# Compression of a paged cache: the loop over batch rows unrolled and staggered by component, both chunk halves summed in one PSUM bank, and small vectors of the front loaded as rows

## The chip, the cores and the metric

The kernel runs on one NeuronCore of one Trainium2 chip. The metric is the device time of one launch in microseconds (us), the median of several runs; lower is better.

## What is computed

One decoder layer for a prompt of 1024 tokens and for 8 samples of one token, each with 4096 cached tokens in pages. Two of its parts matter here. The **front** makes modulation vectors from the conditioning (`silu(c) @ w_ada + b_ada`), normalizes the tokens, modulates them and multiplies them by the input projection; a short convolution over three tokens follows on a part of its columns. The **compression** turns each 32 cached raw key or value rows (stride 16) into one row by a small MLP:

```python
chunks = kv_raw.reshape(B, n_chunk, 16, 2, N_KV_HEADS, 64)
w1 = cmp_w1.reshape(2, CMP_CHUNKS, 16, 64, 128)          # CMP_CHUNKS = 2 halves
proj = einsum('bnsckd,crsdh->bnrckh', chunks, w1)
hid = proj[:, :n, 0] + proj[:, 1:n + 1, 1]                # half 0 of a chunk + half 1 of the next
bias = einsum('cld,cldh->ch', cmp_pos, cmp_w1) + cmp_b1
hid = gelu(hid + bias)
comp = einsum('bnckh,chd->bnckd', hid, cmp_w2) + cmp_b2   # keys are rotated afterwards
```

It runs for 8 samples (256 chunks each) and for the prompt (64 chunks). There are four components for each: key or value, times two heads. Attention, a mixture of experts and the final norm follow and aren't touched.

## The kernel before

The kernel is a row of stages with a barrier between them: `fro` (the front), `cmp` (compression), `att`, `smp`, the merge and routing, `moe`, `fin`. Each engine has its own program; they meet at semaphores. fp32 numbers are split into a high part (`h`, type fp32r) and a remainder (`l`), and each product is three fp32r matmuls.

**Front (`stage_front`).** SP loads four 2 MB pieces of `w_ada` (three buffers), then pieces of `w_in`. POOL loads the nine token tiles (512 KB each) into four buffers; between tiles 2 and 3 it issues five loads of small vectors (`biasT`, `gT`, `wconv`) as columns, elements of 4 bytes. PE makes `condition(n)` (16 fp32 matmul instructions), then transposes two token tiles, four times; the last, 8-row tile comes at the end. ACT and DVE then split the first 8 blocks of weights, and ACT makes the modulated high part `xh` with scale and bias in one pass while DVE makes the modulated fp32 value and the remainder `xl`. 12 convolution groups and 27 groups of `z` (three blocks of columns, nine token tiles) follow. The results of `z` go out through two buffers, so group m waits for the store of group m-2 (L609). The last rows for the convolution state leave from POOL as six transfers of 4-byte elements (L300, L302).

**Compression (`stage_compress`).** For sample i, POOL gathers two halves of 128 chunks, 2 MB each, into `x0`, `x1`. ACT and DVE copy them into `xs` by component (`shuffle`); PE transposes 4 blocks at a time into one of four banks (16 such groups for a sample, L901); ACT copies each to `xh` (L768), DVE writes the remainder `xl` (L838) and thereby frees the bank. `product` is 48 fp32r matmuls of 256 columns (L911) for a component; the two chunk halves go to two parts of a bank, and DVE adds them with a shift of one column (L846, L848), then ACT makes the gelu (L786). `second` is the fp32 product with `w2`: for keys two matmuls, the second with rotated columns (L881, L882), for values one for each half (L887). `keys` and the rows at L855 finish the output. The order within a sample is written out:

```python
return (turn[0:8] + nxt[0:1] + turn[8:12] + [("product", 0)] + turn[12:14] + [("product", 1)]
        + turn[14:16] + nxt[1:2] + [("product", 2), ("product", 3)])
```

Sample 0 is unrolled, 1 to 7 are in a hardware loop (the last one partly outside, on ACT and DVE), and the prompt is a ninth pass with 64 columns. Before all this SP loads the page table in eight pieces and the positions as columns (4-byte elements), then tables and weights, the first-layer weight `w1` (2 MB) last, and right behind it a 4 MB copy in HBM (`o_win_s`). PE makes the position bias with 32 fp32 matmuls of one column (L869).

## Time and profile before

| what | value |
|---|---|
| median of 3 runs | 2507.45 us (2501.72 to 2516.19) |
| the profiled execution | 2502.97 us |
| its span, first to last instruction | 2501.2 us |
| mean granted TensorE clock | 0.876 |
| front | 0 to 349 us |
| compression, set-up until its first product | 352 to 418 us |
| compression, 8 samples | 418 to 725 us |
| compression, prompt | 725 to 773 us |

The profiled execution is one run; what is worked out from its rows is measured against its own time. Busy time of PE is modelled (matmuls are pipelined), so the distance between the starts of two matmuls is the better measure of their cost. PEclk is the share of full clock that was granted: 1.00 is 2.4 GHz, 0.50 is 1.2 GHz.

### The profile page before, as it was taken

To read this page: it belongs to the slowest core of one execution; us is meant where nothing else is said; L and a number is where in the kernel's file an instruction comes from. 1 tells how busy PE (TensorE), PEld (TensorE's weight loads), DVE (VectorE), ACT (ScalarE), POOL (GpSimd) and SP (SyncE) were. 2 spreads that over 40 slices of the span, in tenths; PEclk is the share of its full clock that TensorE was granted. 3 is DMA by queue.
4 is the path that set the end of the run, shared out by engine and by line. 5 is a ranking of instruction groups with operands and counts; after the bars stand their busy time and mean duration, and the time that the engine had idled before them with its cause. 6 is when DMAs were issued, how large, how long until landed. Compare 5 with 4: busy or idle time off the path is not lost. (4 is left out here: it accounts for less than half of the span.)

```text
span 2501.2 us, 29798 instructions
## 1 busy us (share of the span) xinstructions
...
## 2 busy tenths in 40 slices
...
GB/s 271 95 70 16 84 111 202 117 128 113 58 5 87 228 23 17 5 5 17 129 164 225 33 299 89 77 48 320 425 426 415 415 416 411 415 335 275 194 52 287
DMA packets 168247, 444.13 MB, mean 178 GB/s; under 512 B 49157, under 2 KB 96227, under 8 KB 136397
## 3 DMA queue, kind: packets, MB, share of 16 engines
...
q14 instruction: 34, 0.28, 0.0%
...
## 5 line engine op out<-in xcount | busy, mean ns | idle before, releaser
L2626 DVE TENSOR_TENSOR moe_lo<-wts_raw,moe_hi 128x2048 fp32r<-128x2048 f32 x216 | 484.4, 2287 | 59.8 <-ACT moe_hi L2541 59.7
L2541 ACT ACTIVATE moe_hi<-wts_raw 128x2048 fp32r<-128x2048 f32 x216 | 401.3, 1915 | 25.2 <-PE moe_U L2423 25.2
L911 PE MATMUL cmp_hp<-cmp_xh,cmp_wh 128*128 128x256 f32 (+1 forms) x576 | 177.0, 307 | 16.5 <-DVE cmp_xl L838 16.5
L911 PE MATMUL cmp_hp<-cmp_xh,cmp_wl 128*128 128x256 f32 (+1 forms) x576 | 174.0, 302 | 0.0
L911 PE MATMUL cmp_hp<-cmp_xl,cmp_wh 128*128 128x256 f32 (+1 forms) x576 | 173.9, 302 | 0.0
L2409 PE MATMUL moe_G<-moe_hi,moe_xh 128*128 128x512 f32 x288 | 117.6, 408 | 44.0 <-DVE moe_lo L2626 36.3
L2449 PE MATMUL moe_Y<-moe_hi,moe_hh 128*128 128x512 f32 x288 | 118.6, 412 | 29.4 <-DVE moe_hl L2642 24.9
L911 PEld LDWEIGHTS cmp_hp<-cmp_xh,cmp_wh 128*128 128x128 f32 x576 | 122.9, 213 | 21.8 <-issue 19.2
L1309 ACT ACTIVATE att_prow<-att_S,att_low 128x640 f32<-128x640 f32 (+15 forms) x192 | 107.7, 563 | 46.5 <-DVE att_low L1367 43.8
L1299 ACT ACTIVATE att_ph<-att_pT 128x512 fp32r<-128x512 f32 (+5 forms) x148 | 88.3, 597 | 87.1 <-PE att_pT L1207 86.8
L911 PEld LDWEIGHTS cmp_hp<-cmp_xh,cmp_wl 128*128 128x128 f32 x576 | 123.1, 214 | 0.0
L911 PEld LDWEIGHTS cmp_hp<-cmp_xl,cmp_wh 128*128 128x128 f32 x576 | 123.1, 214 | 0.0
L1352 DVE TENSOR_TENSOR att_pl<-att_pT,att_ph 128x512 fp32r<-128x512 f32 (+5 forms) x148 | 101.5, 689 | 35.7 <-ACT att_ph L1299 33.6
L2450 PE MATMUL moe_Y<-moe_hi,moe_hl 128*128 128x512 f32 x288 | 116.9, 406 | 0.0
L2451 PE MATMUL moe_Y<-moe_lo,moe_hh 128*128 128x512 f32 x288 | 116.5, 405 | 0.0
L2410 PE MATMUL moe_G<-moe_hi,moe_xl 128*128 128x512 f32 x288 | 116.2, 404 | 0.0
L2411 PE MATMUL moe_G<-moe_lo,moe_xh 128*128 128x512 f32 x288 | 116.1, 403 | 0.0
L786 ACT ACTIVATE cmp_hid<-cmp_raw,cmp_bias 128x255 f32<-128x255 f32 (+1 forms) x36 | 17.7, 491 | 231.5 <-DVE cmp_raw L848 231.5
L2421 PE MATMUL moe_U<-moe_hi,moe_xh 128*128 128x512 f32 x288 | 115.0, 399 | 0.0
L2423 PE MATMUL moe_U<-moe_lo,moe_xh 128*128 128x512 f32 x288 | 112.4, 390 | 0.0
L2422 PE MATMUL moe_U<-moe_hi,moe_xl 128*128 128x512 f32 x288 | 112.3, 390 | 0.0
L1367 DVE TENSOR_REDUCE att_low<-att_S 128x1 f32<-128x640 f32 (+14 forms) x184 | 98.3, 547 | 20.9 <-PE att_S L1240 19.3
...
## 6 DMA issues: line engine op xcount, KB each, us to landing
...
```

What stands on the lines that cost most here:

```text
L911: last = pe.matmul(hp[k % 2][:, r, 0:cols], lhs[:, w, :], rhs[:, k, t, 0:cols], start=(t == 0 and m == 0), stop=(t == 7 and m == 2))
L2409: pe.matmul(G[:, :], xh[k][:, c, :], wh, start=(c == 0), stop=False)
L2410: pe.matmul(G[:, :], xl[k][:, c, :], wh, start=False, stop=False)
L2411: last = pe.matmul(G[:, :], xh[k][:, c, :], wl, start=False, stop=(c == KT - 1))
L2421: pe.matmul(U[:, :], xh[k][:, c, :], wh, start=(c == 0), stop=False)
L2422: pe.matmul(U[:, :], xl[k][:, c, :], wh, start=False, stop=False)
L2423: last = pe.matmul(U[:, :], xh[k][:, c, :], wl, start=False, stop=(c == KT - 1))
L2449: pe.matmul(Y[part][:, :], hh[:, c, :], wh, start=(c == 0), stop=False)
L2450: pe.matmul(Y[part][:, :], hl[:, c, :], wh, start=False, stop=False)
L2451: last = pe.matmul(Y[part][:, :], hh[:, c, :], wl, start=False, stop=(c == KD - 1))
L2541: act.activation(hi[p][half][:, :], raw[p][half][:, :], ACT.Copy).then_inc(hi_ready[p], 1)
L2626: dve.tensor_tensor(lo[p][half][:, :], raw[p][half][:, :], hi[p][half][:, :], ALU.subtract).then_inc(lo_ready[p], 1)
```

## The change

In the front, the small vectors and the convolution's weights arrive as 36 rows and are transposed by PE (`cols`, `colT`); they and `state_conv` are issued behind the first `w_ada` piece, and token tiles 2 and 3 wait for that piece. Token tiles are transposed 2, 3, 3 and 1 at a time. The modulation is made by DVE alone (`modulate`), ACT then only copies the high part. The ends of the convolution are gathered in `endT`, transposed by PE after the first group of `z`, copied by ACT and stored by SP as rows.

In the compression, 32 steps u = 4i + c (sample, component) are unrolled. In step u PE does `product(u)`, then `turn(u + 2)` and `second(u - 1)`; the copies for u + 4 follow. `xh` and `xl` hold three components. Both chunk halves accumulate in one bank, the second reading its columns one element later (`t * TS + r`). The positions are two extra columns of steps 0 and 2, the prompt's 64 chunks are extra columns of the last four steps (320 in all). Keys take one matmul of 128 output rows. The page indices are spread by a small matmul; `w1` comes as two halves in the gather buffer of sample 1 and is loaded early; the copy `o_win_s` is issued after sample 0.

The diff, cut:

```diff
-        biasT = s.sb("biasT", [P, 2 * KT])
-        gT = s.sb("gT", [P, KT])
+        NCOL = 3 * KT + 3 * CJ
+        cols = s.sb("cols", [NCOL, P])
+        colT = s.sb("colT", [P, NCOL])
+        biasT, gT = colT[:, 0:2 * KT], colT[:, 2 * KT:3 * KT]
+        wconv = colT[:, 3 * KT:NCOL].rearrange("p (r j) -> p r j", r=3)
         modT = s.sb("modT", [P, 2 * KT, 9])
...
-            for n in range(NRAW):
+            load_raw(0)
+            sp.dma_start(cols[0:2 * KT, :], a["b_ada"][0, 0:2 * D].rearrange("(k p) -> k p", p=P)).then_inc(st_in, 16)
+            sp.dma_start(cols[2 * KT:3 * KT, :], a["ln1_g"][0].rearrange("(k p) -> k p", p=P)).then_inc(st_in, 16)
+            sp.dma_start(cols[3 * KT:NCOL, :], a["w_conv"][0].rearrange("r (j p) -> (r j) p", p=P)).then_inc(st_in, 16)
+            sp.dma_start(st[:, :], a["state_conv"][0].rearrange("b r n -> (b r) n")).then_inc(st_in, 16)
+            for n in range(1, NRAW):
                 load_raw(n)
-            sp.dma_start(st[:, :], a["state_conv"][0].rearrange("b r n -> (b r) n")).then_inc(st_in, 16)
             for n in range(NRAW, ADA1 + NRAW):
...
+            sp.wait_ge(tails_kept, 1)
+            sp.dma_start(a["o_conv_p"][0, 0], ends[0:2, :]).then_inc(row_out, 16)
+            sp.dma_start(a["o_conv_s"][0, :, 1, :], ends[2:2 + NB, :]).then_inc(row_out, 16)
...
+                if t == 2:
+                    pool.wait_ge(w_in[0], 16)
                 if t >= 4:
                     pool.wait_ge(turned, t - 3)
                 src = a["x_prompt"][0, t * P:(t + 1) * P, :] if t < NT else a["x_sample"][:, 0, :]
                 pool.dma_start(x[t % 4][0:n, :], src).then_inc(x_in[t % 4], 16)
-                if t == 2:
-                    with nc.allow_non_contiguous_dma(reason="columns of small vectors"):
-                        pool.dma_start(biasT[:, :], a["b_ada"][0, 0:2 * D].rearrange("(k p) -> p k", p=P)).then_inc(const_in, 16)
-                        pool.dma_start(gT[:, :], a["ln1_g"][0].rearrange("(k p) -> p k", p=P)).then_inc(const_in, 16)
-                        for r in range(3):
-                            pool.dma_start(wconv[:, r, :], a["w_conv"][0, r].rearrange("(j p) -> p j", p=P)).then_inc(const_in, 16)
...
-            pool.wait_ge(tails, CJ)
-            with nc.allow_non_contiguous_dma(reason="rows of conv state"):
-                for r in range(2):
-                    pool.dma_start(a["o_conv_p"][0, 0, r].rearrange("(j p) -> p j", p=P), tail[:, :, r]).then_inc(end_out, 16)
-                for j in range(CJ):
-                    pool.dma_start(a["o_conv_s"][0, :, 1, j * P:(j + 1) * P].rearrange("b p -> p b"), vsT[:, j, :]
-                                   ).then_inc(end_out, 16)
-            pool.wait_ge(end_out, 16 * (2 + CJ))
...
+        turns = [(0, 1), (2, 3, 4), (5, 6, 7), (8,)]
...
-            act.wait_ge(kept_v, TT)
-            act.wait_ge(mod_ready, 2)
+            for k in range(KT):
+                act.wait_ge(h_ready, k + 1)
+                act.activation(xh[:, k, 0:T], raw[:, k, 0:T], ACT.Copy).then_inc(h_high, 1)
+            act.wait_ge(h_ready, KT + 1)
             act.activation(xh[:, :, T:W], raw[:, :, T:W], ACT.Copy).then_inc(h_high, 1)
-            for k in range(KT):
-                act.activation(xh[:, k, 0:T], raw[:, k, 0:T], ACT.Identity, bias=modT[:, k, NB:9],
...
-                turn(2 * n)
-                turn(2 * n + 1)
+                for t in turns[n]:
+                    turn(t)
...
+            def modulate(k):
+                dve.tensor_scalar(raw[:, k, 0:T], raw[:, k, 0:T], modT[:, KT + k, NB:9], modT[:, k, NB:9],
+                                  ALU.mult, ALU.add).then_inc(h_ready, 1)
+                dve.wait_ge(h_ready, k + 1)
+
+            modulate(0)
+            for k in range(KT):
+                if k + 1 < KT:
+                    modulate(k + 1)
+                else:
+                    step(dve.tensor_tensor(raw[:, :, T:W], raw[:, :, T:W], modT[:, KT:, 0:NB], ALU.mult))
+                    dve.tensor_tensor(raw[:, :, T:W], raw[:, :, T:W], modT[:, 0:KT, 0:NB], ALU.add).then_inc(h_ready, 1)
+                    dve.wait_ge(h_ready, KT + 1)
+                dve.wait_ge(h_high, k + 1)
+                dve.tensor_tensor(xl[:, k, 0:T], raw[:, k, 0:T], xh[:, k, 0:T], ALU.subtract).then_inc(h_split, 1)
...
+    def cols(u):
+
+        if u in (0, 2):
+            return NCH + 2
+        return NCH if u < NU - 4 else TS
+
...
+    order = [("shuffle", 0), ("shuffle", 1), ("turn", 0), ("turn", 1), ("shuffle", 2), ("shuffle", 3)]
+    for u in range(NU):
+        order.append(("product", u))
+        if u + 2 < NU:
+            order.append(("turn", u + 2))
+        if u + 4 < NU:
+            order.append(("shuffle", u + 4))
...
+        x = [[s.sb(f"x{i}{h}", [P, 16 * 4 * HD]) for h in range(2)] for i in range(2)]
+        xs = [[s.sb(f"xs{i}{h}", [P, 16, HD]) for h in range(2)] for i in range(2)]
+        xp = s.sb("xp", [PCH, 4, 16, HD])
+        xh = s.sb("xh", [P, 3, 8 * TS + 2], F32R)
+        xl = s.sb("xl", [P, 3, 8 * TS + 2], F32R)
...
-            return (turn[0:8] + nxt[0:1] + turn[8:12] + [("product", 0)] + turn[12:14] + [("product", 1)]
-                    + turn[14:16] + nxt[1:2] + [("product", 2), ("product", 3)])
...
+            sp.dma_start(pages[:, :], a["page_table"]).then_inc(page_in, 16)
+            sp.dma_start(ident[:, :], a["c_ident"]).then_inc(page_in, 16)
+            sp.dma_start(spread[:, :, :], a["c_pages"]).then_inc(page_in, 16)
+            sp.dma_start(c8[:, :], a["c_mod8"]).then_inc(page_in, 16)
+            sp.dma_start(pos[:, :], a["cmp_pos"][0].rearrange("c (t l) d -> (c t) (l d)", l=2)).then_inc(page_in, 16)
+            for k in range(2):
+                sp.dma_start(w1[:, 16 * k:16 * k + 16, :],
+                             a["cmp_w1"][0, k].rearrange("(t l) d h -> (l d) t h", l=2)).then_inc(w_in[k], 16)
...
+            prompt = a["o_cmp_p"][0, 0].rearrange("(n s) k g d -> n (k g) s d", s=16)
+            for c in range(4):
+                sp.dma_start(xp[:, c, :, :], prompt[:, c, :, :]).then_inc(prompt_in, 16)
+            for b in range(NB):
+                if b == 1:
+                    sp.dma_start(a["o_win_s"][0, :, 0:511].rearrange("b (x y) c g d -> b x (y c g d)", y=7),
+                                 a["cache_win_kv"][0, :, 1:512].rearrange("b (x y) c g d -> b x (y c g d)", y=7)
+                                 ).then_inc(win_out, 16)
...
+                    if i == 1 and h == 0:
+                        pool.wait_ge(w_split, 2)
+                    if i >= 2:
+                        pool.wait_ge((shuffled_a, shuffled_v)[h], 4 * (i - 2) + 4)
+                    pool.indirect_dma_start(x[i % 2][h][:, :], None, chunks,
+                                            bass.IndirectOffsetOnAxis(ap=idx[:, h, i:i + 1], axis=0)).then_inc(x_in[i % 2][h], 16)
...
+            def second(u):
+                i, c = u // 4, u % 4
+                n = max(NCH, cols(u)) if i else NCH
+                pe.wait_ge(hid_ready, u + 1)
+                if c < 2:
+                    pe.wait_ge(k_done, 2 * i + c)
+                    pe.matmul(kp[:, 0:n], w2k[:, :], hid[:, u % 2, 0:n], start=True, stop=True).then_inc(k_psum, 1)
...
+            def product(u):
+                c = u % 4
+                n = cols(u)
+                pe.wait_ge(free, turned_to(u))
+                if u >= 2:
+                    pe.wait_ge(hid_ready, u - 1)
+                if u == 0:
+                    pe.wait_ge(pos_ready, 1)
+                if u in (0, 2):
+                    pe.wait_ge(w_split, u // 2 + 1)
+                for r in range(2):
+                    for t in range(8):
+                        w = 16 * (c // 2) + 8 * r + t
+                        at = slice(t * TS + r, t * TS + r + n)
+                        for m, (lhs, rhs) in enumerate(((wh, xh), (wl, xh), (wh, xl))):
+                            last = pe.matmul(hp[u % 2][:, 0:n], lhs[:, w, :], rhs[:, u % 3, at],
+                                             start=(r == 0 and t == 0 and m == 0), stop=(r == 1 and t == 7 and m == 2))
+                last.then_inc(product_done, 1)
...
+            for what, n in order:
+                if what == "turn":
+                    turn(n)
+                    if n == 2:
+                        pe.wait_ge(const_in, 16 * NCONST)
+                        pe.wait_ge(w2_ready, 1)
+                    elif n > 2:
+                        second(n - 3)
+                elif what == "product":
+                    product(n)
+                    if n + 2 >= NU:
+                        second(n - 1)
...
+            def keep(v):
+                for m, (v_, h, t0) in enumerate(turns):
+                    if v_ != v:
+                        continue
+                    act.wait_ge(turned, m + 1)
+                    if v >= 3:
+                        act.wait_ge(product_done, v - 2)
+                    n = parts(v)[h]
+                    copy(xv[:, v % 3, t0:t0 + 4, h * P:h * P + n], bank[m % 4][:, :, 0:n]).then_inc(high, 1)
...
+            def gelu(u):
+                i, c = u // 4, u % 4
+                n = cols(u) if i else NCH
+                act.wait_ge(product_done, u + 1)
+                if u in (0, 2):
+                    act.wait_ge(bias_ready, u // 2 + 1)
+                if u >= 2:
+                    j, d = (u - 2) // 4, (u - 2) % 4
+                    act.wait_ge((k_psum, v_psum)[d // 2], 2 * j + d % 2 + 1)
+                act.activation(hid[:, u % 2, 0:n], hp[u % 2][:, 0:n], ACT.Gelu_apprx_tanh, bias=bias[:, c // 2:c // 2 + 1]
+                               ).then_inc(hid_ready, 1)
...
-                        dve.tensor_copy(raw[k % 2][:, 0:n], hp[k % 2][:, 0, 0:n]).then_inc(added, 1)
-                        dve.wait_ge(added, 4 * i + k + 1)
-                        dve.tensor_tensor(raw[k % 2][:, 0:n], raw[k % 2][:, 0:n], hp[k % 2][:, 1, 1:n + 1],
-                                          ALU.add).then_inc(raw_ready, 1)
```

**DVE in the compression.** Before, from the transposed groups before the first product to the one before the third (`cmp_xl` is the remainder, `cmp_raw` the sum of the halves):

```order
L838 TENSOR_TENSOR cmp_xl<-cmp_bank,cmp_xh 128x4x128 x8
L706 COPY cmp_xs<-cmp_x 128x1024 x2
L838 TENSOR_TENSOR cmp_xl<-cmp_bank,cmp_xh 128x4x128 x4
L846 COPY cmp_raw<-cmp_hp 128x255
L848 TENSOR_TENSOR cmp_raw<-cmp_raw,cmp_hp 128x255
L838 TENSOR_TENSOR cmp_xl<-cmp_bank,cmp_xh 128x4x128 x2
L846 COPY cmp_raw<-cmp_hp 128x255
L848 TENSOR_TENSOR cmp_raw<-cmp_raw,cmp_hp 128x255
L838 TENSOR_TENSOR cmp_xl<-cmp_bank,cmp_xh 128x4x128 x2
L706 COPY cmp_xs<-cmp_x 128x1024 x2
```

Now, two steps behind one another (`cmp_t`, `cmp_ck` finish keys, `cmp_cv` values, `cmp_xs` is the copy by component):

```order
L924 SCALAR_TENSOR_TENSOR cmp_t<-cmp_kp,cmp_b,cmp_rope 64x256
L926 SCALAR_TENSOR_TENSOR cmp_t<-cmp_kp,cmp_b,cmp_rope 64x256
L928 TENSOR_TENSOR cmp_ck<-cmp_t 64x256
L917 TENSOR_TENSOR cmp_xl<-cmp_bank,cmp_xh 128x4x128 x4
L737 COPY cmp_xs<-cmp_x 128x1024
L924 SCALAR_TENSOR_TENSOR cmp_t<-cmp_kp,cmp_b,cmp_rope 64x256
L926 SCALAR_TENSOR_TENSOR cmp_t<-cmp_kp,cmp_b,cmp_rope 64x256
L928 TENSOR_TENSOR cmp_ck<-cmp_t 64x256
L917 TENSOR_TENSOR cmp_xl<-cmp_bank,cmp_xh 128x4x128 x4
```

The twelve remainders ahead of a product are gone from there; each step has four remainders and one copy for later steps, and the two adding instructions on `cmp_raw` no longer exist.

**SP at the head of the compression.** Before:

```order
L714 DMA cmp_pt<-in_page_table 16x16x1 x8
L715 DMA cmp_pos<-in_cmp_pos 128x32x1
L716 DMA cmp_b<-in_cmp_b 128x2x1
L718 DMA cmp_b<-in_cmp_b 64x1
L719 DMA cmp_b<-in_cmp_b 32x1
L720 DMA cmp_b<-in_cmp_b 32x1
L721 DMA cmp_ident<-in_c_ident 128x128
L722 DMA cmp_rope<-in_c_ropec 64x510
L723 DMA cmp_b2v<-in_cmp_b 128x64
L724 DMA cmp_w<-in_cmp_w 128x2x64
L725 DMA cmp_w<-in_cmp_w 128x32x128
L727 DMA o_win_s<-in_cache_win_kv 8x8x16352
```

Now, behind the page table, the identity, the spreading table and `c8`:

```order
L745 DMA cmp_pos<-in_cmp_pos 32x128
L747 DMA cmp_x<-in_cmp_w 128x16x128 x2
L750 DMA cmp_b<-in_cmp_b 128x2x1
L752 DMA cmp_b<-in_cmp_b 64x1
L753 DMA cmp_b<-in_cmp_b 32x1
L754 DMA cmp_b<-in_cmp_b 32x1
L755 DMA cmp_rope<-in_c_ropec 128x320
L756 DMA cmp_b2v<-in_cmp_b 128x64
L757 DMA cmp_w<-in_cmp_w 128x2x64
L758 DMA cmp_w2k<-in_cmp_w 128x32
L759 DMA cmp_w2k<-in_cmp_w 128x32
L762 DMA cmp_xp<-o_cmp_p 64x16x64 x4
```

`w1` (`in_cmp_w` 128x16x128, twice) moved ahead of the small tables, the column loads of pages and positions are gone, four loads of the prompt's rows are new, and the copy `o_win_s` is no longer here.

**PE at the end of the front's first part** (`fro_wraw` x8 is `condition`, `fro_xbuf` a token tile, `fro_mrow` the modulation). Before:

```order
L406 MATMUL fro_tp<-fro_ident,fro_xbuf 128x128 x16
L413 MATMUL fro_ps<-fro_ident,fro_mrow 128x9 x4
L396 MATMUL fro_ps<-fro_wraw,fro_cT 9x512 x8
L406 MATMUL fro_tp<-fro_ident,fro_xbuf 128x128 x16
L413 MATMUL fro_ps<-fro_ident,fro_mrow 128x9 x8
L406 MATMUL fro_tp<-fro_ident,fro_xbuf 128x8 x8
L439 MATMUL fro_ps<-fro_xh,fro_wh 128x344
```

Now:

```order
L398 MATMUL fro_ps<-fro_wraw,fro_cT 9x512 x8
L408 MATMUL fro_tp<-fro_ident,fro_xbuf 128x128 x24
L415 MATMUL fro_ps<-fro_ident,fro_mrow 128x9 x4
L398 MATMUL fro_ps<-fro_wraw,fro_cT 9x512 x8
L408 MATMUL fro_tp<-fro_ident,fro_xbuf 128x8 x8
L415 MATMUL fro_ps<-fro_ident,fro_mrow 128x9 x8
L441 MATMUL fro_ps<-fro_xh,fro_wh 128x344
```

Two more token tiles stand ahead of the last `condition`, and the small one now stands ahead of the last turns of the modulation, whose end the first product waits for.

## Rows read from the trace of the kernel before

**Rows 1.** The page of the kernel before, its first line.

```profile
span 2501.2 us, 29798 instructions
```

**Rows 2.** Compression by stage: window, length, busy time (instructions) of PE to POOL, PEclk, DMA, GB/s.

```profile
504.50:527.00 22.50, 21.42 (x170) 19.93 (x167) 9.70 (x22) 5.94 (x10) 0.94 (x1) 1.00 0.27 100
527.00:538.50 11.50, 9.21 (x64) 7.36 (x65) 8.92 (x16) 8.34 (x15) 0.94 (x1) 0.97 0.17 40
725.00:773.00 48.00, 47.03 (x238) 46.05 (x237) 7.21 (x26) 4.45 (x12) 0.00 (x0) 0.51 0.02 4
```

**Rows 3.** DVE in order of time, compression: start, us, line, names, x, [idle before].

```profile
425.74 0.42 DVE L846 COPY cmp_raw<-cmp_hp 128x255 f32<-128x255 f32 x1 [6.42 <-PE cmp_hp L911]
...
432.36 0.42 DVE L846 COPY cmp_raw<-cmp_hp 128x255 f32<-128x255 f32 x1 [3.39 <-PE cmp_hp L911]
...
701.67 0.42 DVE L846 COPY cmp_raw<-cmp_hp 128x255 f32<-128x255 f32 x1 [6.47 <-PE cmp_hp L911]
...
723.08 0.42 DVE L846 COPY cmp_raw<-cmp_hp 128x255 f32<-128x255 f32 x1 [4.69 <-PE cmp_hp L911]
```

**Rows 4.** PE in order of time, compression, four places.

```profile
418.18 0.43 PE L911 MATMUL cmp_hp<-cmp_xh,cmp_wh 128*128 128x256 f32 x1 [2.00 <-DVE cmp_xl L838]
418.41 0.42 PE L911 MATMUL cmp_hp<-cmp_xh,cmp_wl 128*128 128x256 f32 x1
...
428.20 0.28 PE L911 MATMUL cmp_hp<-cmp_xh,cmp_wh 128*128 128x256 f32 x1
428.32 0.28 PE L911 MATMUL cmp_hp<-cmp_xh,cmp_wl 128*128 128x256 f32 x1
...
510.72 0.64 PE L881 MATMUL cmp_kp<-cmp_hid,cmp_w 128*64 128x255 f32 x2
511.20 0.59 PE L882 MATMUL cmp_kp<-cmp_hid,cmp_w2r 128*64 128x255 f32 x2
...
728.91 0.40 PE L911 MATMUL cmp_hp<-cmp_xl,cmp_wh 128*128 128x64 f32 x1
729.12 0.40 PE L911 MATMUL cmp_hp<-cmp_xh,cmp_wh 128*128 128x64 f32 x1
```

**Rows 5.** Groups by line and shape, compression, ACT and DVE: xcount, busy us, mean ns.

```profile
L768 ACT ACTIVATE cmp_xh<-cmp_bank 128x512 fp32r<-128x512 f32 x128 | 69.2, 597 | 23.6 <-PE cmp_bank L901 23.6
L768 ACT ACTIVATE cmp_xs<-cmp_x 128x1024 f32<-128x1024 f32 x32 | 32.0, 1054 | 25.4 <-DMA cmp_x<-in_cache_cmp_kv,cmp_idx 25.4
L786 ACT ACTIVATE cmp_hid<-cmp_raw,cmp_bias 128x255 f32<-128x255 f32 x32 | 16.3, 509 | 189.7 <-DVE cmp_raw L848 189.7
...
L838 DVE TENSOR_TENSOR cmp_xl<-cmp_bank,cmp_xh 128x512 fp32r<-128x512 f32 x128 | 79.8, 684 | 28.7 <-ACT cmp_xh L768 28.6
L706 DVE COPY cmp_xs<-cmp_x 128x1024 f32<-128x1024 f32 x32 | 20.6, 686 | 14.2 <-DMA cmp_x<-in_cache_cmp_kv,cmp_idx 14.2
```

**Rows 6.** The same stage view over 50 us of the front, 344 columns a matmul.

```profile
100.00:150.00 50.00, 50.00 (x320) 50.00 (x319) 22.10 (x49) 10.01 (x20) 0.00 (x0) 1.00 0.22 75
```

**Rows 7.** ACT in order of time at the head of the compression.

```profile
370.08 2.00 ACT L768 ACTIVATE cmp_xs<-cmp_x 128x1024 f32<-128x1024 f32 x2 [21.65 <-DMA cmp_x<-in_cache_cmp_kv,cmp_idx]
375.82 2.00 ACT L768 ACTIVATE cmp_xs<-cmp_x 128x1024 f32<-128x1024 f32 x2 [3.73 <-DMA cmp_x<-in_cache_cmp_kv,cmp_idx]
393.90 3.62 ACT L773 ACTIVATE cmp_wh<-cmp_w 128x4096 fp32r<-128x4096 f32 x1 [16.08 <-DMA cmp_w<-in_cmp_w]
```

**Rows 8.** PE in order of time at the beginning of the front.

```profile
17.90 9.26 PE L396 MATMUL fro_ps<-fro_wraw,fro_cT 128*9 128x512 f32 x16 [12.88 <-DMA fro_wraw<-in_w_ada]
...
71.47 0.62 PE L439 MATMUL fro_ps<-fro_xh,fro_wh 128*128 128x344 f32 x1 [9.25 <-DVE fro_xl L551]
```

**Rows 9.** PE in order of time between two groups of z.

```profile
268.68 0.76 PE L439 MATMUL fro_ps<-fro_wh,fro_xh 128*128 128x512 f32 x1 [6.26 <-DVE fro_wl L509]
```

**Rows 10.** Waits of DVE between 220 and 300 us: total, times, longest.

```profile
DVE fro_arena L609 <- DMA s_z<-fro_arena: 26.0, 2, 20.4
```

**Rows 11.** The stage view over four us after the stop of group 9.

```profile
268.00:272.00 4.00, 3.32 (x9) 2.69 (x10) 4.00 (x7) 0.00 (x0) 0.00 (x0) 0.55 0.18 70
```

475 lines of the change are left out of this document (218 added, 257 removed).

## The prediction

> **What bounds the kernel now.** I read the page first, then the stage view, to see where TensorE (PE) is full and where it waits. The span is 2501.2 us [rows 1]; the profiled execution took 2502.97 us, 4.5 us below the median of 2507.45 us. The stages are separated by barriers, so time taken out of the front or the compression goes out of the total one for one, and the stages behind stay as they are.
>
> The compression has three faults of its own. (1) Its nine passes are not full. The reader should take the start of the first adding copy of sample 0, 425.74, and of sample 7, 701.67: seven samples in 275.93 us, 39.4 us each [rows 3]. Inside a sample PE is full from 504.5 to 527, at full clock, while from 527 to 538.5 it is busy 9.2 of 11.5 us with transposes that wait for ACT and DVE [rows 2]. (2) The prompt's pass takes 48 us, with PE busy 47 of them at a granted clock of 0.51 [rows 2]: its matmuls start 0.21 us apart though they have only 64 columns, no faster than 256 columns at the low clock, 0.23 us [rows 4]. (3) The head: the gathered halves are there at 370.08 and 375.82, but the weight lands at 393.90 [rows 7], and the first product starts at 418.18 [rows 4].
>
> In the front, PE has nothing to multiply until the first piece of `w_ada` lands at 17.90, and the first projection matmul is at 71.47 [rows 8]. Later DVE waits 26.0 us in two waits for stores of `z` [rows 10], is late with a weight split, and PE stands 6.26 us [rows 9], after which the mean clock over four us is 0.55 [rows 11].
>
> **The steps of the compression.** A matmul of 256 columns costs 0.12 us [rows 4], so one product is 48 x 0.12 = 5.76 us. Between the adding copies of components 0 and 1 lie 6.62 us [rows 3], that is one product and 8 transposes, so 8 transposes cost 0.86 us and the 16 of a component 1.72 us. A key's second matmul costs 0.48 us (510.72 to 511.20 [rows 4]); one of two goes. For a value's four narrow matmuls I take the same 0.5. A component then needs 5.76 + 1.72 + 0.5 = 7.98 us of PE. Before, four components needed about 4 x 7.98 + 2 x 0.48 = 32.9 us of the 39.4.
>
> PE reaches these 7.98 us only if nothing in a step is late. ACT does four copies, one shuffle and one gelu: 4 x 0.60 + 1.05 + 0.51 = 3.9 us. DVE does four remainders and one shuffle, 4 x 0.68 + 0.69 = 3.4 us, and an output of up to three instructions of a size with the copy of rows 3, 0.42 us, 4.7 in all [rows 5]. Both are well inside 7.98, and the order gives them a whole product of lead: turns run two components ahead, their bank is freed during the product, the gelu that `second` needs is a product old, and the two adding instructions on DVE have gone. The adding itself I count as no gain: its 0.84 us a component are DVE's, beside a product of 5.76; only if DVE became the bound would its going be worth that much. The gathers (4 MB for 32 us) are doubled, so each has a sample's time; two 2 MB halves came 5.74 us apart [rows 7]. The 4 MB copy blocks SP's queue behind sample 0's stores; SP's next duty is the store of sample 1's keys, some 30 us later.
>
> Sum from the first product: 32 x 5.76 = 184.3; turns 30 x 1.72 = 51.6 (two are ahead of the first product); second 32 x 0.5 = 16. The prompt's 64 extra columns: 344 columns cost 50 / 320 = 0.156 us [rows 6], so 64 more columns cost 0.026 us, times 192 = 5.0; its transposes 1.7 (between 0 and 3.4, the price of full ones). The start at the low clock: 418.18 to 425.74 is 7.56 instead of 5.76, so 1.8. The last output 1.9, as from 723.08 to 725 now [rows 2, 3]. Together **262.3 us** against 773 - 418.2 = 354.8 now: **-92.5**.
>
> The head: `w1` is issued some ten us earlier on SP, ahead of the small tables, and without the 4 MB copy; 2 MB cost about 5.7 us. The indices take one more hop (two transposes and a matmul on PE), against eight column loads less. So the last wait becomes the second gathered half. It can come at 372 (less traffic) or at 382 (the prompt's rows, 1 MB in small pieces, beside it); I keep the 375.8 of now plus 1. Behind it are two DVE copies, four remainders and the turns between: 2 x 0.69 + 4 x 0.68 and a us for PE, 5 us. The position bias on PE, the long split and 48 transposes are no longer between. First product at 382 instead of 418.2: **-36** (-31 to -41).
>
> **The steps of the front.** The first `w_ada` piece shares the DMA engines with two token tiles instead of four and with none of the element loads: 3 MB at 5.7 us for 2 MB is 8.6 us, from about 3.5, so it lands at 12 instead of 17.9. I take -5.5 (0 if the elements cost nothing, at most -9). PE's work after it is the same but for one small transpose; the last tile moves ahead of the final modulation turn, and DVE's `modulate(0)` replaces a wait for ACT: -0.5. The products that follow are PE's own pace. In `z` the element stores are gone, DVE is no longer late: -6.3, and -1.8 of clock (4 us at 0.55 [rows 11]); four transposes more, +0.4. The ends of the convolution wait for one group of `z` on ACT, which has nothing else there, and SP's first store of `z` waits about as long for its own group. Front: **-13.7** (-5 to -18).
>
> Total -92.5 - 36 - 13.7 = -142. 2503 - 142 = 2361; the median lies 4.5 higher, so **2365 us**.
>
> **The rivals.**
> - *A step has a hidden wait.* A handshake each step (PE's first bank, the gelu's wait for the matmul two steps back, a wait on DVE's chain) of 1 us costs 32 us: 2397. For it: PE lost about 2 us in 527 to 538.5 to this very chain [rows 2]; against it: the lead of one product.
> - *The clock falls in the turns.* Rows 2 show 1.00 over 22.5 us with 16 transposes between products, and 0.97 where 48 transposes stood with gaps, so I don't expect it. If each turn let it fall, a step would lose the 1.8 us of a cold start [rows 3, 4]: 32 x 1.8 = 58, so 2423. The Trainium skill ("TensorE: Matmul & The Clock Gate", Part 4: PE-mode transpose) says that transposes don't count as work for the clock; by that rule the time would be this one, and the trace speaks against it in short turns.
> - *The shifted half is read at half rate.* The second half's columns start one element on, which no matmul here does now. If it costs double: 24 x 32 x 0.12 = 92, so 2457.
> - *It falls into the slow gear: slower than before.* The 64-column matmuls show such a gear: 0.21 us for 64 columns at the low clock [rows 2, 4], four times the price of a column. At full clock 256 columns would cost 0.21 x 4 / 2 = 0.42, 0.30 more, times 768 = 230 us: 2595. It decides from 142 / 768 = 0.185 us more a matmul. Nothing in the trace hints at it but the gear itself; 256 columns and more aren't in it.
> - *The head and front move little.* Loads land no earlier than now because the rate and not the order bounds them: `w_ada` at 17.9 and the second half at 387. 5.5 + 11 less, so 2382.
>
> **How the numbers follow.** Forecast 0.76, hidden wait 0.08, clock 0.06, half rate 0.03, slow gear 0.03, early loads 0.04. The range 2342 to 2400: down by 5 of the head, 4 of the front, 2 of the turns and 12 for steps closer than my distances (0.4 us each, as a value's second product can be half); up to the hidden wait and the late loads. The clock, half rate and gear stay outside, 0.12, and some 0.08 of the forecast's tails. About 0.5% (12.5 us) is what a measurement can tell from no change. Faster by more: all but the gear, 0.97. The gear near its point of decision gives 0.01 for the same, the rest 0.02 slower.
>
> **What would show it.** Right: the first product of the compression about 36 us earlier after the front's end, adding copies gone, `product` every 8.0 us, PEclk 1.00 throughout, the last four products 7.0 us each, PE's wait in `z` gone, compression 292 us from 352 (421 now). Wrong: a step well over 8.2 us (see which wait), matmuls of the shifted half further apart than 0.12, a clock under 1.00 in the turns, the first product waiting for `w1` or for the prompt's rows, or ACT waiting long for a gather.

## The result and the profile after

The changed kernel takes 2383.64 us (median of 4 runs, 2378.95 to 2386.85), the kernel before beside it on the same chip 2511.0 us (4 runs, 2501.72 to 2516.19). The ratio is 0.949 with a 95% interval of 0.946 to 0.952. The forecast was 2365 us with a range of 2342 to 2400; it holds, 18.6 us above the point. The profiled execution took 2384.1 us, where the sum had said 2361.

The page of the kernel after, its first line; it answers to [rows 1]:

```profile
span 2382.3 us, 28748 instructions
```

The stage view of the kernel after: the end of the head, the start of the products, and the steps up to the prompt's (window, length, busy time and instructions of PE, PEld, DVE, ACT, POOL, then PEclk, DMA share, GB/s). It answers to [rows 2]:

```profile
366.00:371.70 5.70, 5.02 (x24) 5.02 (x25) 5.18 (x8) 2.84 (x5) 0.00 (x0) 0.50 1.16 327
371.70:380.00 8.30, 8.30 (x68) 8.30 (x67) 2.86 (x7) 4.15 (x6) 1.87 (x2) 0.94 1.09 359
...
420.00:604.00 184.00, 183.35 (x1537) 181.94 (x1536) 89.40 (x176) 78.28 (x138) 9.03 (x8) 1.00 0.32 121
```

PE is full from the first product on. In the 184 us from 420 on it stands 0.65 us, at a granted clock of 1.00, though 16 transposes lie between any two products. The stretch of 48 us at 0.51 is gone: the prompt's 64 columns ride in the bank of the last sample. The rival of the clock falling in the turns is answered in this view alone.

The gelus of the kernel after in order of time (start us, length, engine, line, shapes, count, idle before). One stands behind each product, so their distance is a step:

```profile
441.44 0.47 ACT L892 ACTIVATE cmp_hid<-cmp_hp,cmp_bias 128x256 f32<-128x256 f32 x1 [4.49 <-PE cmp_hp L841]
...
584.20 0.47 ACT L892 ACTIVATE cmp_hid<-cmp_hp,cmp_bias 128x256 f32<-128x256 f32 x1 [4.48 <-PE cmp_hp L841]
...
593.58 0.47 ACT L892 ACTIVATE cmp_hid<-cmp_hp,cmp_bias 128x256 f32<-128x256 f32 x1 [5.07 <-PE cmp_hp L841]
...
604.21 0.53 ACT L892 ACTIVATE cmp_hid<-cmp_hp,cmp_bias 128x320 f32<-128x320 f32 x1 [6.33 <-PE cmp_hp L841]
...
614.87 0.53 ACT L892 ACTIVATE cmp_hid<-cmp_hp,cmp_bias 128x320 f32<-128x320 f32 x1 [7.37 <-PE cmp_hp L841]
...
625.66 0.53 ACT L892 ACTIVATE cmp_hid<-cmp_hp,cmp_bias 128x320 f32<-128x320 f32 x1 [7.49 <-PE cmp_hp L841]
633.22 0.53 ACT L892 ACTIVATE cmp_hid<-cmp_hp,cmp_bias 128x320 f32<-128x320 f32 x1 [7.04 <-PE cmp_hp L841]
```

From 441.44 to 584.20 lie 18 steps: 7.93 us each, forecast 7.98. In these steps, of samples 2 to 6, nothing else sets the pace; `[4.48 <-PE cmp_hp L841]` is ACT waiting for PE. With the prompt's columns a step takes 10.6 to 10.8 us, and the last, which has no turns beside it, 7.56.

The head, in order of time over all engines; it answers to [rows 4, 7]:

```profile
340.04 0.28 DVE L624 TENSOR_TENSOR fro_arena<-fro_arena 8x128 f32<-8x128 f32 x1
...
352.34 1.91 ACT L871 ACTIVATE cmp_wh<-cmp_x 128x2048 fp32r<-128x2048 f32 x1 [12.98 <-DMA cmp_x<-in_cmp_w]
...
358.34 1.91 ACT L871 ACTIVATE cmp_wh<-cmp_x 128x2048 fp32r<-128x2048 f32 x1 [4.09 <-DMA cmp_x<-in_cmp_w]
...
360.83 2.00 ACT L871 ACTIVATE cmp_xs<-cmp_x 128x1024 f32<-128x1024 f32 x2 [0.58 <-DMA cmp_x<-in_cache_cmp_kv,cmp_idx]
...
365.93 1.30 DVE L737 COPY cmp_xs<-cmp_x 128x1024 f32<-128x1024 f32 x2 [3.35 <-DMA cmp_x<-in_cache_cmp_kv,cmp_idx]
...
371.72 0.56 PE L841 MATMUL cmp_hp<-cmp_xh,cmp_wh 128*128 128x258 f32 x1
```

The gathered halves land at 360.83 and 365.93 and the first product starts at 371.72 (418.18 before, [rows 4]). The weight's halves land at 352.34 and 358.34 and are split before the second gathered half is there, so the weight is off the path.

The front: PE in order of time; it answers to [rows 8]:

```profile
12.46 9.64 PE L398 MATMUL fro_ps<-fro_wraw,fro_cT 128*9 128x512 f32 x16 [7.54 <-DMA fro_wraw<-in_w_ada]
...
34.37 1.06 PE L408 MATMUL fro_tp<-fro_ident,fro_xbuf 128*128 128x128 f32 x8 [0.83 <-DVE fro_arena L507]
37.20 1.06 PE L408 MATMUL fro_tp<-fro_ident,fro_xbuf 128*128 128x128 f32 x8 [1.77 <-ACT fro_arena L323]
...
51.58 8.73 PE L398 MATMUL fro_ps<-fro_wraw,fro_cT 128*9 128x512 f32 x16
```

`w_ada` lands at 12.46 instead of 17.90. But the third transposes of a group wait 1.77 us (and 1.75 once more, in the next group), and the last modulation product takes 8.73 us where it took 7.04, as this line of the kernel before shows:

```profile
50.81 7.04 PE L396 MATMUL fro_ps<-fro_wraw,fro_cT 128*9 128x512 f32 x16
```

The first projection matmul starts at 69.45, only 2.0 us earlier than in [rows 8].

Between the compression's last output and the next stage, all engines in order of time:

```profile
635.51 0.48 DVE L936 TENSOR_TENSOR cmp_cv<-cmp_vp,cmp_b2v 128x64 f32<-128x64 f32 x3 [1.07 <-PE cmp_vp L823]
636.01 0.65 SPq L772 DMA_DIRECT2D s_cv<-cmp_cv  x2
636.71 0.96 SPq L773 DMA_DIRECT2D s_ck<-cmp_ck  x1
637.71 0.51 SPq L774 DMA_DIRECT2D s_cv<-cmp_cv  x1
...
642.56 0.06 DVE L1463 MEMSET att_ckt<- 128x2 f32 x1 [6.58 <-PEq L84]
```

DVE waits 6.58 us for the next stage. In the kernel before, at the same place:

```profile
775.45 0.06 DVE L1402 MEMSET att_ckt<- 128x2 f32 x1 [2.57 <-PEq L84]
```

The last stores stand behind the last output, and the stage ends when they have landed. There are four now (64.0, 63.5, 31.5 and 31.5 KB); before there was one of 31.5 KB.

Stage by stage, against the profiled execution of the kernel before (PE's last matmul of the front, DVE's last output of the compression, PE's first and last turning matmul of the attention, PE's first projection matmul of the merge, DVE's last output; each read from the tile's own view):

| stage | before | after | difference |
|---|---|---|---|
| front, to PE's last matmul | 347.8 | 338.7 | -9.1 |
| compression, to its last output | 424.9 | 297.1 | -127.8 |
| to the attention's first matmul | 9.6 | 13.5 | +3.9 |
| attention of the prompt | 388.6 | 395.4 | +6.8 |
| attention of the samples | 298.3 | 303.9 | +5.6 |
| merge, experts, final | 1027.5 | 1028.8 | +1.3 |

The two parts that the change touches most gave 136.9 us, and 17.6 of them are gone behind them, 12.4 in two stages whose instructions are the same. Where those went is what most of the experiments are about.

### The profile page after: what moved, and what is told of

Its sections match the earlier page's. It is cut to its first block and busy times, and to the rows that moved or that the text cites. A ratio compares the mean times of both kernels' runs of the same rounds, so it can differ in the third digit from the quotient of the medians.

```text
span 2382.3 us, 28748 instructions
## 1 busy us (share of the span) xinstructions
PE 1986.7 (83%) x10585; PEld 1579.7 (66%) x10585; DVE 1341.0 (56%) x2058; ACT 1052.4 (44%) x1605; POOL 110.6 (5%) x107
## 5 line engine op out<-in xcount | busy, mean ns | idle before, releaser
L917 DVE TENSOR_TENSOR cmp_xl<-cmp_bank,cmp_xh 128x512 fp32r<-128x512 f32 (+1 forms) x136 | 82.6, 668 | 121.1 <-ACT cmp_xh L871 121.0
L841 PE MATMUL cmp_hp<-cmp_xh,cmp_wh 128*128 128x256 f32 (+2 forms) x512 | 150.5, 294 | 0.0
L841 PE MATMUL cmp_hp<-cmp_xh,cmp_wl 128*128 128x256 f32 (+2 forms) x512 | 147.0, 287 | 0.0
L841 PE MATMUL cmp_hp<-cmp_xl,cmp_wh 128*128 128x256 f32 (+2 forms) x512 | 146.9, 287 | 0.0
L1428 DVE TENSOR_REDUCE att_low<-att_S 128x1 f32<-128x640 f32 (+14 forms) x184 | 98.7, 548 | 21.7 <-PE att_S L1301 18.9
L441 PE MATMUL fro_ps<-fro_xh,fro_wh 128*128 128x344 f32 x288 | 93.6, 325 | 9.9 <-DVE fro_xl L565 8.0
L1268 PE MATMUL att_pT<-att_ident,att_prow 128*128 128x128 f32 (+7 forms) x592 | 98.5, 292 | 3.8 <-DVE att_pl L1413 2.5
L841 PEld LDWEIGHTS cmp_hp<-cmp_xh,cmp_wh 128*128 128x128 f32 x512 | 97.7, 191 | 0.5
```

The lines of the kernel that those rows point to most:

```text
L841: last = pe.matmul(hp[u % 2][:, 0:n], lhs[:, w, :], rhs[:, u % 3, at], start=(r == 0 and t == 0 and m == 0), stop=(r == 1 and t == 7 and m ...
```

## The experiments

Twelve further runs were made in three groups, each group on one chip with the kernel before beside it, which took 2520.2, 2518.1 and 2515.6 us; times are best read as ratios.

### The two parts alone

The compression as changed with the front as it was: function `stage_front` of the kernel before in the changed kernel.

> The compression as changed, the front as it was. By the two traces the compression's last output came 136.9 us earlier and the front's end 9.1 us earlier, so the compression itself gained 127.8 us; some 4 us of it went back at the stage's end, where the last stores are now waited for. Theory A: the 14 us that the attention and sample stages took longer in the changed kernel's profile are their own (the granted clock there varies from one execution to the next), so the gain against the kernel before is 124 us give or take 6, and the stages of this run show another pattern of clock than either. Theory B: the loss comes with the compression's new end (what it leaves in the queues, or the clock it leaves behind): the gain is 110 us and the same stages show the same dips of the clock as in the changed kernel. Theory C: it comes with the front; then 124 us here with the clock of the kernel before in those stages.

The ratio was 0.950 (0.948 to 0.952), 2395.6 us against 2520.2: -124.6. That is the number of theories A and C, and B's 110 is outside the interval (121 to 132 us). C wanted the clock of the kernel before in the later stages, but the attention took 400.2 us in this trace and 388.6 in that one, so A is left. The reverse, `stage_front` of the changed kernel in the kernel before:

> The front as changed, the compression as it was. Theory A: 9 us less than the kernel before (between 6 and 12, since the front ended 9.1 us earlier and nothing behind it is bound to it). Theory B: the two parts lean on each other (the loads of the compression follow the front's last stores), so the two single gains don't add up to the gain of the whole, 127 us. If the later stages' clock is a matter of where in time they begin, this run, 9 us ahead of the kernel before, may show dips that neither other run has.

The ratio was 0.993 (0.991 to 0.995), 2504.6 us: -15.6, more than the 9 us expected, with an interval that reaches from 12.9 to 21.7 us (0.9949 and 0.9914 times 2520.2). In its trace the front ended at 341.1, 6.7 us earlier than in the kernel before, so the rest lies behind the front; what made it is not shown, the later stages' own scatter (below) is large enough. The sum of both, 140 us, stands against a gain of the whole of 127 us in the first comparison and 136 in the repeat below; with intervals of 4 to 9 us to either side of each number this shows no loss from putting the two together.

### The pace of the steps

Does the lead of one product fill PE, or would one bank and fewer adding copies have done it?

```
-    order = [("shuffle", 0), ("shuffle", 1), ("turn", 0), ("turn", 1), ("shuffle", 2), ("shuffle", 3)]
+    order = [("shuffle", 0), ("shuffle", 1)]
     for u in range(NU):
+        order.append(("turn", u))
+        if u + 2 < NU:
+            order.append(("shuffle", u + 2))
         order.append(("product", u))
-        if u + 2 < NU:
-            order.append(("turn", u + 2))
-        if u + 4 < NU:
-            order.append(("shuffle", u + 4))
```

> The changed kernel with the order turn, shuffle, product: the turns of a component stand right ahead of its own product, with no component between. Theory A (the pipelining is what fills PE): in the changed kernel the last remainder of a component ends 3.8 us after its first transpose, and the product could start 2.0 us after it, so PE would stand about 1.8 us in each of 31 steps: 56 us, 2440 us in place of 2384 (2425 to 2460, the upper end if the standing lets the clock fall, 1.8 us more in some steps); the head is some 3 us shorter, as only one component is turned ahead. Theory B (the gain comes from fewer adding copies and one bank, the lead does nothing): under 10 us more.

It took 2431.0 us, a ratio of 0.966 (0.962 to 0.970), 48.7 us more than the changed kernel on that chip, where 56 were expected; 2431 lies in the stated 2425 to 2460. The waits of PE in its compression, from 378 to 695 us (engine, line, what it waited for: us in total, times, longest):

```profile
PE cmp_hp L840 <- DVE cmp_xl L916: 47.1, 31, 4.5
```

31 waits of 1.5 us in the mean, 47.1 in all, for the last remainder: theory A. A step took 9.68 us (19 steps between the gelus at 410.58 and 594.52) instead of 7.93, 1.75 more, where 1.8 had been expected. To its last output the compression took 358.5 us instead of 297.1, so the order is worth 61.4 us of the stage by the traces; the whole shows 48.7 because the two later stages were short in this run (691.0 us together, 699.7 in the changed kernel's repeat). Whether the waits cost clock as well:

```profile
380.00:420.00 40.00, 32.46 (x248) 31.41 (x249) 15.34 (x29) 12.74 (x23) 2.19 (x2) 0.91 0.30 111
420.00:600.00 180.00, 151.21 (x1241) 145.96 (x1241) 73.81 (x143) 65.37 (x114) 10.94 (x10) 1.00 0.38 147
600.00:640.00 40.00, 33.93 (x269) 32.85 (x268) 15.20 (x31) 13.76 (x24) 0.00 (x0) 0.96 0.03 7
640.00:696.00 56.00, 50.12 (x349) 46.69 (x348) 18.56 (x43) 15.12 (x31) 0.00 (x0) 0.97 0.03 8
```

Over 180 us they did not, at 1.00 with PE busy in 151.2 of 180 us; at both ends the clock stood at 0.91, 0.96 and 0.97, where the changed kernel has 1.00.

The other half of the question, the adding copies put back between product and gelu:

```
-                act.wait_ge(product_done, u + 1)
+                act.wait_ge(raw_ready, u + 1)
...
+                    dve.wait_ge(product_done, n + 1)
...
+                    step(dve.tensor_copy(raw[:, n % 2, 0:m], hp[n % 2][:, 0:m]))
+                    dve.tensor_tensor(raw[:, n % 2, 0:m], raw[:, n % 2, 0:m], hp[n % 2][:, 0:m], ALU.max).then_inc(raw_ready, 1)
```

> The changed kernel with two DVE instructions between each product and its gelu put back, a copy out of the bank and a maximum with the bank (which leaves the values as they are), as the kernel before had a copy and an addition there. Theory A (the adding copies were never the cost, the lead hides them): 32 x 0.84 = 27 us more of DVE beside PE, and the time the same within 0.3%. Theory B (their going is part of the gain): up to 27 us more, 2411. If the turns' copies on ACT, which stand behind the gelu, get late, PE shows waits at the transposes of some 0.8 us in each component; that is theory B's sign.

The ratio was 0.949 (0.943 to 0.955), the median 2388.7 us, and the interval is too wide for 0.3%. The trace says more than the time. Its groups by line and shape, from 378 to 635 us (counts, busy us, mean ns, idle before), and PE's waits there:

```profile
L987 DVE COPY cmp_raw<-cmp_hp 128x256 f32<-128x256 f32 x28 | 11.9, 424 | 54.3 <-PE cmp_hp L843 54.3
L988 DVE TENSOR_TENSOR cmp_raw<-cmp_raw,cmp_hp 128x256 f32<-128x256 f32 x28 | 11.8, 421 | 1.0
```

```profile
PE cmp_bank L812 <- DVE cmp_xl L919: 4.5, 4, 1.2
```

DVE does 26.7 us more (with 3.0 us for the three of 320 columns), and PE waits 4.5 us in four waits, all for a free bank at the turns with the prompt's rows, which are six groups on four banks. From the first product to the last it took 267.5 us against 261.2: the two instructions cost 6.3 us of 27. Nearly all of it is in the steps with the prompt's rows: the 18 steps from the gelu at 441.94 to that at 584.75 take 7.93 us each, as without them. Theory A holds for the steps without the prompt, B for the four steps where a turn waits for DVE.

The odd first column:

```
-                        at = slice(t * TS + r, t * TS + r + n)
+                        at = slice(t * TS, t * TS + n)
```

> The changed kernel with the second half of each product read from the same first column as the first half, not one on; so the position of a token half within a chunk is wrong in the compressed keys and values, everything else is computed as before. Theory A (an odd first column costs nothing): the matmuls of 256 columns start 0.118 us apart as now, a component 7.86 us, the same time within 0.3%. Theory B (it costs something that the even spacing hides, such as a first access of two): 768 matmuls by 5 ns or more, at least 4 us less.

The ratio was 0.944 (0.939 to 0.949), too wide again, but the products span 260.8 us in its trace and 261.2 in the changed kernel's: 0.5 ns a matmul. The shifted half costs nothing.

### The front

The same tiles, turned in pairs:

```
-        turns = [(0, 1), (2, 3, 4), (5, 6, 7), (8,)]
+        turns = [(0, 1), (2, 3), (4, 5), (6, 7, 8)]
```

> The changed kernel with the token tiles turned in pairs, as before, and the last group of three with the short tile at its end. Theory A: the groups of three are what ate the front's gain. ACT squares and scales a tile between two copies, so the third turn of a group waited 1.77 and 1.75 us; with pairs each group waits 0.83, which gives back 2.7 us, and the modulation product before the last turns goes from 8.73 to 7.04 us as its clock is whole again: some 4 us less than the changed kernel, the front's first weight split at 57 us instead of 61. Theory B: the token tiles come late because they wait for the first piece of the modulation weight, and the turns would wait in pairs as well: no change, within 1 us. Theory C: the short tile's turn at the end costs what the pairs give.

2376.7 us, a ratio of 0.942 (0.941 to 0.944). The kernel was not run beside the changed one, so its front is read from its trace, PE in order of time:

```profile
34.61 1.06 PE L408 MATMUL fro_tp<-fro_ident,fro_xbuf 128*128 128x128 f32 x8 [0.83 <-DVE fro_arena L507]
...
46.17 7.04 PE L398 MATMUL fro_ps<-fro_wraw,fro_cT 128*9 128x512 f32 x16
...
55.06 1.07 PE L408 MATMUL fro_tp<-fro_ident,fro_xbuf 128*128 128x128 f32 x8 [0.83 <-DVE fro_arena L507]
56.96 0.63 PE L408 MATMUL fro_tp<-fro_ident,fro_xbuf 8*128 8x8 f32 x8 [0.83 <-DVE fro_arena L507]
```

No wait over 0.83 us, 7.04 us for the last modulation product, and the weight splits on ACT start at 57.72 instead of 61.03. The front's last matmul is at 335.4 instead of 338.7: 3.3 us, theory A, somewhat less than its 4. The eight executions with groups of three had their last matmul of the front between 336.7 and 341.1, 339.0 in the mean, the two with pairs at 335.4 and 335.5.

### The end of the compression's stage

```
+                if b == NB - 1:
+                    sp.dma_start(a["s_ck"][NB, :, :, 0:PCH - 1], ck[:, :, NCH:TS - 1]).then_inc(ck_out, 16)
...
+            act.wait_ge(v_done, 2 * NB)
+            act.dma_start(a["s_cv"][NB - 1, P:NCMP, :], cv[0:NCMP - P, 1, :, :].rearrange("p g d -> p (g d)")).then_inc(cv_out, 16)
+            act.dma_start(a["s_cv"][NB, 0:PCH - 1, :], cv[0:PCH - 1, 2, :, :].rearrange("p g d -> p (g d)")).then_inc(cv_out, 16)
```

> The changed kernel with the compression's last stores spread: the prompt's keys stored as soon as they are there, and of the three last stores of values two issued by ACT, one by SP. Theory A: between DVE's last output and the next stage's first instruction lie 6.6 us (2.6 before the change), 2.2 of them in issues on SP; this takes about 2 us (1.2 to 3). Theory B: the landing of a store bounds it, however it is issued: under 0.5 us.

2380.7 us, ratio 0.944 (0.942 to 0.946). The gap was 6.84 us, no shorter: spreading the issues gave nothing, as theory B had it. The transfers themselves ran at 22 to 35 GB/s in its last microseconds, and what was left then could be the store of 127 rows. So it was cut in two, together with the pairs of the front:

```
+            sp.dma_start(a["s_cv"][NB - 1, P + 64:NCMP, :], cv[64:NCMP - P, 1, :, :].rearrange("p g d -> p (g d)")).then_inc(cv_out, 16)
...
-            act.dma_start(a["s_cv"][NB - 1, P:NCMP, :], cv[0:NCMP - P, 1, :, :].rearrange("p g d -> p (g d)")).then_inc(cv_out, 16)
+            act.dma_start(a["s_cv"][NB - 1, P:P + 64, :], cv[0:64, 1, :, :].rearrange("p g d -> p (g d)")).then_inc(cv_out, 16)
```

> Pairs of turns in the front as in the run with pairs, and the compression's last stores spread again, now with the store of 127 rows cut in two (64 on ACT's queue, 63 on SP's), since in the run with the stores spread the traffic after the last output went at 22 to 35 GB/s for some 5 us and the gap stayed at 6.84 us. Theory A: a single store of 127 rows is what lasts; cut in two the gap to the next stage goes to about 4.5 us, and with the 3.3 us of the pairs this kernel is 5.5 us faster than the changed one, 0.23%, at the edge of what five rounds can tell. Theory B: the gap is the landing of any store plus the barrier; then it stays above 6 and only the pairs' 3.3 us are left.

DVE, SP and ACT in order of time at the end of the compression of this kernel:

```profile
634.97 0.48 DVE L940 TENSOR_TENSOR cmp_cv<-cmp_vp,cmp_b2v 128x64 f32<-128x64 f32 x3 [1.07 <-PE cmp_vp L824]
635.48 0.34 SPq L774 DMA_DIRECT2D s_cv<-cmp_cv  x1
635.48 0.51 ACTq L907 DMA_DIRECT2D s_cv<-cmp_cv  x1
635.85 0.35 SPq L775 DMA_DIRECT2D s_cv<-cmp_cv  x1
636.03 0.75 ACTq L908 DMA_DIRECT2D s_cv<-cmp_cv  x1
...
638.92 0.06 DVE L1467 MEMSET att_ckt<- 128x2 f32 x1 [3.47 <-PEq L84]
```

The gap is 3.47 us: theory A, and more of it than expected. The windows over the last transfers show why, first with the store whole, then with it cut (the last two numbers are the share of the 16 DMA engines' time that was busy, and GB/s):

```profile
638.00:640.00 2.00, 0.00 (x0) 0.00 (x0) 0.00 (x0) 0.00 (x0) 0.00 (x0) 0.50 0.07 20
```

```profile
636.30:637.50 1.20, 0.00 (x0) 0.00 (x0) 0.00 (x0) 0.00 (x0) 0.00 (x0) 0.50 0.54 135
```

A share of 0.07 is about one engine of 16 (0.0625), a share of 0.54 more than eight. So the tail with the whole store looks like 127 rows on one engine, one behind the other, and its two parts like transfers spread over many. Other row counts were not tried. With 2372.7 us and 0.944 (0.941 to 0.946) this kernel is ahead of the changed one on the same chip, 2382.3 and 0.947 (0.944 to 0.950), in the median by 9.6 us; the intervals just overlap, so the times alone don't settle it. By the traces the two edits are worth 6.4 us (3.3 and 3.1); the rest is not accounted for. Its compression was 2.6 us longer in the profiled execution, since PE stood 2.9 us at an early turn.

### The two stages behind

The attention took 6.8 us longer, the samples' 5.6. Three windows of the attention's first third in the changed kernel:

```profile
737.00:747.00 10.00, 7.75 (x53) 7.29 (x53) 6.75 (x20) 6.01 (x20) 0.00 (x0) 0.89 0.01 2
747.00:757.00 10.00, 9.76 (x42) 9.06 (x42) 4.63 (x15) 4.29 (x16) 0.00 (x0) 0.50 0.00 1
757.00:767.00 10.00, 8.23 (x53) 7.06 (x51) 6.97 (x16) 6.61 (x18) 0.00 (x0) 0.93 0.00 0
```

The instructions are the same, and so is what PE waits for behind the stage's first matmul: 53.7 us in all in the kernel before, 52.2 in the changed one. What differs is the clock, 0.90 in the mean over the stage before and 0.87 after. From 745 to 758 it stands at 0.50, after PE had stood 1.47 us before 743.43; in the profiled execution of the kernel before the same place was low for 3 us. Is this the change's doing, or an execution's chance? The changed kernel once more, unaltered:

> The changed kernel itself, unaltered, beside the next three on one chip. Theory A (the longer attention stage belongs to this kernel): from the first to the last turning matmul of the attention 395.4 us again, within 1 us, with the clock down in the same places, 93 to 110 us and 130 to 150 us behind the stage's first matmul. Theory B (it varies from one execution to the next): another length, between 388 and 400. The ratio to the kernel before 0.949 again.

The ratio was 0.947 (0.944 to 0.950). The attention took 401.8 us and the sample stage 297.9 us, where the first execution had 395.4 and 303.9. One kernel, two executions, 6 us in either direction: theory B, though 401.8 lies above the 388 to 400 that it gave. With the stage moved by idle work on DVE:

```
+            dve.wait_ge(v_done, 2 * NB)
+            for n in range(7):
+                step(dve.tensor_tensor(wl[:, 0:16, :], wh[:, 0:16, :], wh[:, 0:16, :], ALU.subtract))
```

> The changed kernel with seven subtractions of 2.3 us on DVE behind the compression's last output (nobody uses their result), so that the attention begins some 11.5 us later (16 us less what the last stores' landing took anyway). Theory A (the granted clock of the attention depends on where the dips fall against the work, which a shift moves): the stage's 395.4 us change by 3 to 7 us, and the places where the clock is down move. Theory B (a compression at full rate leaves the attention less clock): the stage stays at 395 or gets shorter by a us for the rest it had. Theory C (it is an execution's chance): the length differs from 395, and from that of the repeat of the changed kernel as much. Total: 2384 + 11.5 and what the stage changes.

The gap grew by 10.6 us and the attention took 400.7 us, the median was 2390.0 us (ratio 0.949, 0.945 to 0.953). With 401.8 us for the unmoved kernel beside it this says nothing about the shift, and the run is inconclusive. That leaves the side of the kernel before, of which there had been one trace:

> The kernel before, unaltered, for the length of its two later stages. With the old compression the attention's turning matmuls spanned 388.6 and 391.3 us, in seven kernels with the new compression 393.2 to 401.8, and the same kernel run twice gave 395.4 and 401.8. Theory A (an execution's chance alone): this run falls anywhere between 388 and 402. Theory B (the new compression costs the attention some 5 us): this run lies at 392 or below. The sample stage, from the attention's last turn to the merge's first projection matmul, is either about 298 or about 305 us in every kernel so far: either of the two here.

> The kernel before once more, for the same two lengths; same expectations as for the first repeat. Together with it, three executions of one kernel then show how far its own lengths vary.

These are single executions; they took 2519.3 and 2512.0 us. The lengths of the two stages over all executions, in us:

| kernel, execution | attention | samples | sum |
|---|---|---|---|
| before, shown in the rows | 388.6 | 298.3 | 686.9 |
| before, first repeat | 396.1 | 308.3 | 704.4 |
| before, second repeat | 396.3 | 302.3 | 698.6 |
| front alone | 391.3 | 304.8 | 696.1 |
| changed | 395.4 | 303.9 | 699.3 |
| changed, repeat | 401.8 | 297.9 | 699.7 |
| compression alone | 400.2 | 305.0 | 705.2 |
| pairs, ends | 395.3, 394.8 | 305.3, 304.1 | 700.6, 698.9 |
| pairs with split stores | 394.4 | 298.4 | 692.8 |
| no lead, idle | 393.2, 400.7 | 297.8, 305.8 | 691.0, 706.5 |
| unshifted, adds | 395.0, 398.5 | 304.3, 294.5 | 699.3, 693.0 |

With the old compression the attention took 388.6 to 396.3 us, with the new one 393.2 to 401.8: the ranges overlap, and theory B of the repeats (392 or below) is out. The mean clock in the two repeats' attention was 0.88. The samples' stage missed its expectation: 308.3 and 302.3 us are neither of the two lengths, nor is the 294.5 of the run with the adding copies. In the sum of both stages, the four executions with the old compression lie at 686.9 to 704.4 with a mean of 696.5, the ten with the new at 691.0 to 706.5 with a mean of 698.6. The execution on which the rows and the sum rest was the shortest of all in these two stages. Of the 12.4 us, 9.6 are its luck (686.9 against the mean of 696.5) and 0.7 the changed execution's; the 2.1 between the two means are far inside the scatter. A few us between the two compressions in the attention alone (means 393.1 and 396.9) can't be excluded with four executions against ten.

## Why the prediction was right, and where it was off

**Steps of the compression, right.** Forecast 262.3 us from the first product to the end, measured 264.3 (371.72 to the last output's end at 636.0). A step took 7.93 us for 7.98, at 0.119 us a matmul (46 distances from 451.52 to 456.98) for 0.12. The match is closer than the terms: the product took 5.9 us for 5.76, the second matmul of a key 0.24 and of a value 0.37 for 0.5, and the errors cancel. No handshake cost anything: PE's only waits there are 0.4 and 0.8 us. One term was too small. The prompt's transposes and columns were put at 1.7 + 5.0; the steps with them came to 9.38, 10.63, 10.66, 10.79 and 7.56 us, which is 11 us over 7.93 (6.2 for the last). The columns cost 0.149 us a matmul (46 distances from 618.47 to 625.31) instead of 0.119, 5.8 us for 192, near the 5.0 of the forecast; the rest is (11.1 - 5.8) / 4 = 1.3 us a component where 0.4 had been put. It stands in the transposes, here in PE's order of time:

```profile
614.67 1.91 PE L810 MATMUL cmp_bank<-cmp_ident,cmp_xs 128*128 128x128 f32 x16
616.69 1.05 PE L810 MATMUL cmp_bank<-cmp_ident,cmp_xp 64*128 64x64 f32 x8
617.67 0.81 PE L819 MATMUL cmp_kp<-cmp_hid,cmp_w2k 128*128 128x320 f32 x2
```

The eight transposes of the prompt's rows take 0.98 us (616.69 to 617.67). At 0.12 us each these 64-row transposes cost as much as the full ones (1.75 us for 16 in the steps before, 0.11 each), so four components come to 3.9 us, just over the upper bound that the forecast had named (3.4). The 16 full ones take 2.02 us here.

**The head, right.** Forecast -36 against the front's end, measured -37.4 (371.72 - 340.32 against 418.18 - 349.39, the ends by DVE's last instruction). The last wait is the second gathered half, as forecast. It landed 9.9 us earlier, 9.1 of which are the front's earlier end; against that end it came 0.8 us earlier than before (25.6 us behind it, 26.4 before), where 1 us later had been put. That the weight, the spread indices and the moved copy each had their part in the 37.4 us is read from the trace; no run takes them apart.

**The front, the mechanism right, a term missed.** Forecast -13.7, measured -9.1. `w_ada` gave 5.4 us (forecast 5.5) and `z` 7.4 (forecast 7.7; PE has no wait of the kind in [rows 9], and DVE none for a store of `z`). The term that failed reads "PE's work after it is the same but for one small transpose". It is the same work in another grouping: the third tile of a group waits for ACT, which squares and scales a tile between two copies. By the run with pairs this ate 3.3 us of the 5.4.

**The end of the stage, not seen.** The sum let the compression end with its last output. It ends with its last store, and the change put four stores behind the last output (190.5 KB), where one of 63 rows (31.5 KB) had stood. This cost 3.9 us; the run with the store of 127 rows cut in two got 3.1 of them back, so most of it is that one store.

**"The stages behind stay as they are", right in the mean, wrong against the one trace.** The sum was made against an execution 4.5 us under the median of three, and that was known; with the fourth run it is 8.0 us under, and that its luck sat in two stages with a varying clock was not known. 12.4 us, 9.6 of them this luck.

With 4.6 for the front, 3.9 for the end, 0.7 for the compression, 12.4 for the two stages and 1.3 behind them, the 23 us between 2361 and 2384.1 are accounted for.

**The rivals.** The hidden wait: none in the steps; the run without lead shows what one would have looked like, 1.5 us in each of 31. The clock falling in the turns: PEclk 1.00 over 184 us of steps. The Trainium skill ("TensorE: Matmul & The Clock Gate", Part 4) says of transposes that they don't count as PE-busy in the same way; this case can only say that a group of 16 (1.75 us) between products lowered nothing. Had it done so in each step, the time would have been 2423. Half rate and slow gear: 0.119 us a matmul over both halves, and the same products read without the shift take 0.5 ns a matmul less. What the slow gear of the 64 columns is stays open: in [rows 2] the weight loads (PEld) are as busy as PE there, 46.05 of 48 us for 237 of them, so its 0.21 us may be theirs and not the columns'; no run tries it. The late loads: `w_ada` landed at 12.46 and the second half at 365.93.
